# Opening two weight groups at once after each residual step of a two-block transformer kernel

## What is computed

```python
# block 1
n = rmsnorm(h, g_pre_mix);  z = n @ w_in                    # 2048 -> 6592 columns
y = concat(short_conv(z), rwkv7(z));  h = h + rmsnorm(y @ w_out, g_post_mix)
gate, up = split(rmsnorm(h, g_pre_ffn) @ w_gate_up)         # 2048 -> 2 x 5632
h = h + rmsnorm((silu(causal_dwconv(gate)) * up) @ w_down, g_post_ffn)
# block 2
q, k, v = split(rmsnorm(h, g0) @ swa_w_in)                  # 2048 -> 3072
h = h + rmsnorm(attention(q, k, v) @ swa_w_out, g1)
gate, up = split(causal_dwconv(rmsnorm(h, g2) @ ffn_w_up))  # 2048 -> 2 x 5632
out = h + rmsnorm((silu(gate) * up) @ ffn_w_down, g3)
```

## Time and profile before

| what | value |
|---|---|
| median of three runs | 2581.58 us (2580.62 to 2581.98) |
| the profiled execution | 2578.3 us, span 2576.5 us |
| TensorE matmul busy | 2443.8 us, 95% |
| VectorE busy | 1533.0 us, 60% |
| ScalarE busy | 1045.8 us, 41% |
| Pool busy | 131.2 us, 5% |
| DMA | 405.84 MB, mean 158 GB/s |
| mean granted TensorE clock | 0.972 |

### The profile page before, as it was taken

The page is one execution under the profiler, slowest core; times in us unless marked ns, Lnnn a source line. Parts: engine busy times, 40 slices in busy tenths (PEclk is TensorE's granted clock), DMA queues, the critical chain, the costliest instruction groups (busy, mean ns, idle before and its releaser), DMA issues.

```text
span 2576.5 us, 51985 instructions
## 1 busy us (share of the span) xinstructions
PE 2443.8 (95%) x20784; PEld 2290.3 (89%) x20784; DVE 1533.0 (60%) x1989; ACT 1045.8 (41%) x1326; POOL 131.2 (5%) x162
## 2 busy tenths in 40 slices
PE   7989999989999999999999898798999999999996
PEld 7989999888899999998887896377999999998885
DVE  6577555655756665564444745545767767774444
ACT  5433232334544434443444434544444444434442
POOL 2001000001200000000000200002100000000001
PEclk9999999999999999999999897799999999999998
DMA  7434232235455555555565562044555555556653
GB/s 237 155 112 135 92 100 92 84 111 186 140 180 183 183 179 186 180 181 188 189 188 177 188 189 81 1 131 132 168 184 187 187 184 184 181 170 203 188 188 98
DMA packets 116212, 405.84 MB, mean 158 GB/s; under 512 B 12624, under 2 KB 19760, under 8 KB 115824
## 3 DMA queue, kind: packets, MB, share of 16 engines
q1 hardware_dynamic: 109248, 392.22, 47.5%
q10 hardware_dynamic: 6832, 11.68, 1.3%
HBM read 401.69 MB, written 2.15 MB: 157 GB/s over the span
## 4 chain that ended last, share of the span: by engine, by line
PE 84%; issue 6%; DVE 6%; ACT 3%; POOL 0%; ACTq 0%; POOLq 0%; DVEq 0%
PE ps L1494 17%; PE ps L1495 17%; PE ps L1496 16%; PE ps L1490 15%; PE ps L1492 7%; PE ps L1615 3%; PE ps L1604 2%; PE ps L1606 1%; PE ps L1605 1%; PE ps L1825 1%; DVE wl L836 1%; ACT wh L493 1%; DVE h L1277 1%; DVE xl L861 1%; DVE rkr L980 1%
## 5 line engine op out<-in xcount | busy, mean ns | idle before, releaser
L836 DVE TENSOR_TENSOR wl<-raw,wh 128x1024 fp32r<-128x1024 f32 x744 | 912.8, 1235 | 836.1 <-ACT wh L493 835.6
L493 ACT ACTIVATE wh<-raw 128x1024 fp32r<-128x1024 f32 x744 | 782.8, 1058 | 1141.4 <-PE ps L1496 670.8
L1494 PE MATMUL ps<-xh,wh 128*128 128x256 f32 (+2 forms) x3648 | 1040.4, 285 | 56.0 <-DVE xl L861 47.0
L1495 PE MATMUL ps<-xl,wh 128*128 128x256 f32 (+2 forms) x3648 | 1036.4, 284 | 0.0
L1496 PE MATMUL ps<-xh,wl 128*128 128x256 f32 (+2 forms) x3648 | 1035.5, 284 | 0.0
L1494 PEld LDWEIGHTS ps<-xh,wh 128*128 128x128 f32 x3648 | 695.1, 191 | 61.2 <-issue 26.3
L1495 PEld LDWEIGHTS ps<-xl,wh 128*128 128x128 f32 x3648 | 696.7, 191 | 0.2
L1496 PEld LDWEIGHTS ps<-xh,wl 128*128 128x128 f32 x3648 | 694.6, 190 | 0.0
L1490 PE MATMUL ps<-act,wh 128*128 128x512 f32 x1408 | 493.1, 393 | 1.6 <-DVE wl L836 1.6
L1492 PE MATMUL ps<-act,wl 128*128 128x256 f32 x1408 | 392.8, 279 | 0.0
L1490 PEld LDWEIGHTS ps<-act,wh 128*128 128x128 f32 x1408 | 263.8, 187 | 64.4 <-DVE wl L836 1.9
(11 more groups left out here) (228 smaller groups left out, 2064.2 us busy)
## 6 DMA issues: line engine op xcount, KB each, us to landing
raw<-in_gate_up SPq DMA_DIRECT2D x176, 512.0 KB, 3.5
raw<-in_down SPq DMA_DIRECT2D x176, 512.0 KB, 3.7
raw<-in_up SPq DMA_DIRECT2D x176, 512.0 KB, 3.6
raw<-in_w_in SPq DMA_DIRECT2D x104, 512.0 KB, 3.6
raw<-in_in SPq DMA_DIRECT2D x48, 512.0 KB, 3.7
raw<-in_w_out SPq DMA_DIRECT2D x32, 512.0 KB, 3.8
raw<-in_out SPq DMA_DIRECT2D x32, 512.0 KB, 3.6
bias<-bias_rows ACTq DMA_DIRECT2D x1, 4096.0 KB, 29.5
```

The lines of the kernel that those rows point to most:

```text
L493: act.activation(wh[:, slot], raw[:, slot], ACT.Copy).then_inc(high_ready, 1)
L836: dve.tensor_tensor(wl[:, slot], raw[:, slot], wh[:, slot].bitcast(F32), ALU.subtract).then_inc(low_ready, 1)
L1494: pe.matmul(out, w_high, hi, start=(k == 0), stop=False)
L1495: pe.matmul(out, w_high, lo, start=False, stop=False)
```

## The change

After each residual step the first two groups of `gate_up`, `in2` and `up2` are opened together. The host lays their 16 chunks down in the order of `TWO`: pair 0 of group 0, pair 0 of group 1, pair 1 of group 0, and so on for six pairs, then pairs 6 and 7 of group 0, then pairs 6 and 7 of group 1. TensorE's `open_two` follows it, with the sum of squares after chunk 13 of the 16. ScalarE and VectorE make two weight chunks behind each pair of tiles from the third pair on, and one more (chunk 16) before the root and reciprocal. The first steps of `gated`, `upped` and `evacuate_in2` wait for other counts of used chunks, and chunks 17 to 23 are placed between them. Pool multiplies by `rstd_post` tiles 1, 3, 4 and all those behind (14 in place of 8); VectorE keeps tiles 0 and 2. The opening of `w_in` and the last residual step stay as they were.

```diff
+TWO = [(g, c) for c in range(6) for g in range(2)] + [(0, 6), (0, 7), (1, 6), (1, 7)]

 (Pool)
                     scale(1)
                     scale(3)
+                    scale(4)
...
-                    with pool.Fori(1, KT // 2 - 1) as i:
+                    with pool.Fori(1, KT // 2 - 2) as i:
                         scale(2 * i + 3)
+                        scale(2 * i + 4)
                         add(2 * i, 0)
                         add(2 * i + 1, 1)
+                    scale(KT - 1)
+                    add(KT - 4, 0)
+                    add(KT - 3, 1)
                     add(KT - 2, 0)
                     add(KT - 1, 1)

 (ScalarE, opening; VectorE's has lows in place of highs)
-                    if c < 3 and first == 0:
+                    if first:
+                        if c >= 2:
+                            highs(first + 2 * c, 2, 2 * c % RING)
+                        continue
+                    if c < 3:
                         highs(1 + c, 1, 1 + c)
-                    if c >= 3:
-                        highs(first + 4 + c - 3, 1, (c - 3) % RING)
-                highs(first + 9, 3, 1)
-                take_root(name)
+                    else:
+                        highs(4 + c - 3, 1, (c - 3) % RING)
+                if first:
+                    highs(first + 16, 1)
+                    take_root(name)
+                    highs(first + 17, 2, 1)

 (ScalarE, feed_forward)
-                pair(0)
+                gated(0)
+                highs(first + 19, 5, 3)
+                activated(0)
+                highs(first + 24, 4)

 (ScalarE, in2)
-            plain("in2", lambda g: None, skip_first=True)
+            highs(FIRST["in2"] + 19, 1, 3)
+            plain("in2", lambda g: None, skipped=2)

 (VectorE, residual_tile)
-                    if k % 2:
-                        dve.wait_ge(scaled_ready, base // 2 + k // 2 + 1)
+                    if k % 2 if name is None else k not in (0, 2):
+                        turn = base // 16 * (KT - 2)
+                        dve.wait_ge(scaled_ready, turn + (k // 2 + 1 if name is None or k < 4 else k - 1))

 (VectorE, gated; upped is the same with lows 21 and 22 between)
+                    opened = isinstance(p, int) and p == 0
...
-                        lows(p * 16 + (first + 13 + x), 1, 1 + x)
-                    dve.wait_ge(chunk_used, p * 16 + (first + 8))
+                        lows(p * 16 + (first + (17 if opened else 13) + x), 1, 1 + x)
+                    dve.wait_ge(chunk_used, p * 16 + (first + (14 if opened else 8)))

 (VectorE, feed_forward)
-                pair(0)
+                gated(0)
+                lows(first + 19, 2, 3)
+                upped(0)
+                lows(first + 23, 1, 3)
+                split(0)
+                lows(first + 24, 4)

 (VectorE, in2)
-            plain("in2", evacuate_in2, skip_first=True)
+            evacuate_in2(0)
+            lows(FIRST["in2"] + 17, 3, 1)
+            plain("in2", evacuate_in2, skipped=2)

 (TensorE)
+            def open_two(name, moving, n):
+                for x, (g, c) in enumerate(TWO):
+                    at_chunk = FIRST[name] + x
+                    chunks_of(name, at_chunk, at_chunk % RING, g, moving[g], n[g], range(c, c + 1),
+                              None if g else tile_ready(name))
+                    if (g, c) == (0, 7):
+                        square_sum(name)
...
-                group(name, 0, 0, x_of(n), n, tile_ready(name))
-                square_sum(name)
-                group(name, 1, 1, x_up, SEQ)
+                open_two(name, (x_of(n), x_up), (n, SEQ))

 (host; the same for in2 and up2)
+    def opened(w):
+        return np.concatenate([w[[8 * g + c for g, c in TWO]], w[16:]])
```

More of the change, by code:

```diff
@@ L526, in opening @@
                     tile(2 * c + 1)
-                    if c < 3 and first == 0:
-                        highs(1 + c, 1, 1 + c)
-                    if c >= 3:
-                        highs(first + 4 + c - 3, 1, (c - 3) % RING)
-                highs(first + 9, 3, 1)
-                take_root(name)
+                    if first:
[3 more added lines that the diff above has]
+                    if c < 3:
+                        highs(1 + c, 1, 1 + c)
+                    else:
[4 more added lines that the diff above has]
+                    highs(first + 17, 2, 1)
+                else:
+                    highs(9, 3, 1)
+                    take_root(name)
             def mix_group(name, g, src, n):
@@ L555, in mix_group, with plain @@
                     square(src[:, k, :], SQ0[name] + k, n)
-            def plain(name, evacuate, skip_first=False, stops={}, ahead=0):
+            def plain(name, evacuate, skipped=0, stops={}, ahead=0):
                 first, per = FIRST[name], CHUNKS[name]
-                for g in range(1 if skip_first else 0, GROUPS[name]):
+                for g in range(skipped, GROUPS[name]):
                     start = first + g * per + RING
@@ L870, in opening, with plain @@
                         finish()
-                    if c < 3 and first == 0:
-                        lows(1 + c, 1, 1 + c)
-                    if c >= 3:
-                        lows(first + 4 + c - 3, 1, (c - 3) % RING)
-                lows(first + 9, 3, 1)
+                    if first:
+                        if c >= 2:
+                            lows(first + 2 * c, 2, 2 * c % RING)
+                        continue
+                    if c < 3:
+                        lows(1 + c, 1, 1 + c)
+                    else:
+                        lows(4 + c - 3, 1, (c - 3) % RING)
+                if first:
+                    lows(first + 16, 1)
+                else:
+                    lows(9, 3, 1)
                 inverse_root(name, rstd)
-            def plain(name, evacuate, skip_first=False, stops={}, middles={}, ahead=0):
+            def plain(name, evacuate, skipped=0, stops={}, middles={}, ahead=0):
                 first, per = FIRST[name], CHUNKS[name]
-                for g in range(1 if skip_first else 0, GROUPS[name]):
+                for g in range(skipped, GROUPS[name]):
                     start = first + g * per + RING
@@ L902, in group_full @@
             def group_full(name, g):
-                ahead = 4 if (name, g) == ("w_out", 0) else 0
+                ahead = {("w_out", 0): 4, ("in2", 0): 6}.get((name, g), 0)
                 dve.wait_ge(chunk_used, FIRST[name] + (g + 1) * CHUNKS[name] + ahead)
@@ L1779, in _ @@
             down("down", 0)
-            group("in2", 0, 0, x_of(SEQ), SEQ, tile_ready("in2"))
-            square_sum("in2")
-            group("in2", 1, 1, x_of(SEQ), SEQ)
+            open_two("in2", (x_of(SEQ), x_of(SEQ)), (SEQ, SEQ))
             with pe.Fori(1, 3) as i:
@@ L1926 @@
         "ht": hidden.T.reshape(KT, P, L).transpose(1, 0, 2),
-        "w_in": _chunks(np.concatenate(columns, axis=1)), "w_out": w_out, "gate_up": _chunks(gate_up),
-        "down": _chunks(a["w_down"]), "in2": _chunks(in2), "out2": _chunks(out2), "up2": _chunks(up2),
+        "w_in": _chunks(np.concatenate(columns, axis=1)), "w_out": w_out, "gate_up": opened(_chunks(gate_up)),
+        "down": _chunks(a["w_down"]), "in2": opened(_chunks(in2)), "out2": _chunks(out2), "up2": opened(_chunks(up2)),
         "down2": _chunks(a["ffn_w_down_2"][0]),
```

## The result

The changed kernel takes 2556.53 us (median of four runs, 2554.43 to 2558.34), the kernel before beside it 2581.78. The ratio is 0.9902, 95% interval 0.9885 to 0.9919: 25 us less. 2559.3 was forecast. The profiled execution took 2558.0 us, with a span of 2556.2.

A forecast was written before the change was run, and what follows sets the result against it. TensorE, busy 95%, was taken to lose time waiting for xl and to its clock. Recoverable 25.6 less costs 1.1, 1.4 and 0.8 gave 22.3 us, from a median of 2581.6 to 2559.3 us; range 2554 to 2573.

The forecast's parts named there:

- Recoverable: First groups of gate_up, in2 and up2: 8.8, 8.7 and 8.1 us of tile waits and clock loss, together 25.6 us.
- a second fall of the clock: TensorE's clock falling again after waits for tiles inside the first groups; counted within the recoverable 25.6 us.
- Part 1: TensorE's new order of the same 16 chunks and 384 matmuls: cost 0, if tiles and weight chunks keep up.
- Part 2: VectorE's chain in the openings: 6.54 us a pair against TensorE's 5.67, lead nearly enough; cost 1.1 us.
- Part 3: Pool's scale of tile 4 disturbs the first xl: each opening starts 0.45 us later, cost 1.4 us in three.
- Part 4: Behind the opening: chunk 19 waits behind the Silu on ScalarE; cost 0.8 us in up2, 0 in gate_up.
- The sum: Whole kernel: 25.6 - 1.1 - 1.4 - 0.8 = 22.3 us less, giving a median of 2559.3 us.
- the signs named ahead: Trace after: 16-chunk openings of 48 to 49 us, waits for xl about 31 us, clock full from 7 us on.
- Pool holding VectorE four times a pair: Openings: each of Pool's four operations delays VectorE, 7.7 us a pair; about 2573 us, chance 0.26.
- The slower rival: Openings: six collisions a pair, 8.9 us, past the deciding point of 8.5 us; 2592 us, chance 0.04.
- No weight chunk was late in an opening: Rival claiming a weight chunk, not a tile, is late in the openings: 2 us a pair, 2570 us, chance 0.03.

The follow-up runs named there:

- The spare matmuls in the kernel before: Kernel before with ten unused matmuls of 256 columns ahead of each of the last five chunks of the three first groups: 2582.17 us, ratio 1.0002.
- the two kernels with longer pairs: Changed kernel with one or two unused VectorE subtractions more per pair of tiles behind pairs 2 to 6 of each opening: 2571.61 and 2589.23 us.

## Why the prediction was right, point by point

- **Recoverable, 25.6 us.** The three openings gave back 26.7. I took the clock's loss at the start as a cost that stays, 7.0 us, and all else as recoverable. For the sum that holds: after the change the openings are 14 chunks and little else, with 2.1, 1.6 and 2.5 us over (42.4 - 40.3, 41.3 - 39.7, 42.2 - 39.7), and (1 - clock) x length is 2.1, 1.7 and 2.5. So 6.2 us stayed and not 7.0. The 0.8 is in2's start, 1.6 against 2.4 before; it was 2.5 again with Pool's scale late, so this part of the gain is luck and not the change. What was not sound is the reading of the time before, as waits and a second fall of the clock. The spare matmuls in the kernel before took the second fall away, and no group was shorter. The start didn't count there either: its 1.7 to 2.9 us were followed in each group by 4.7 to 6.3 us of waits for xl. So the chain set 33.5 to 33.8 us whatever the clock lost. After the change TensorE sets the length, and there the start of the clock does count, but only 0.9 to 1.1 us of it can be had in gate_up and up2 and nothing in in2, since VectorE's chain stands right behind.
- **Part 1.** Nothing was added: 384 matmuls, the same DMA bytes.
- **Part 2, a pair of 6.54 us and 1.1 us of waits.** The pair and its collisions are in VectorE's and Pool's timelines of in2:

```profile
1417.93 0.94 DVE L882 SCALAR_TENSOR_TENSOR xl<-h,vec,xh 128x256 fp32r<-128x256 f32 x1
...
1440.11 2.90 DVE L857 TENSOR_TENSOR wl<-raw,wh 128x1024 fp32r<-128x1024 f32 x2 [1.44 <-ACT wh L501]
1442.94 0.95 DVE L1306 SCALAR_TENSOR_TENSOR h<-mixf,vec,h 128x256 f32<-128x256 f32 x1
...
1446.51 2.90 DVE L857 TENSOR_TENSOR wl<-raw,wh 128x1024 fp32r<-128x1024 f32 x2 [1.44 <-ACT wh L501]
...
1452.44 2.36 DVE L857 TENSOR_TENSOR wl<-raw,wh 128x1024 fp32r<-128x1024 f32 x2 [1.44 <-ACT wh L501]
```

```profile
1415.90 2.69 POOL L438 TENSOR_TENSOR mixf<-mixf,rstd_post 128x256 f32<-128x256 f32 x3 [61.54 <-DVE rstd_post L876]
...
1440.12 3.49 POOL L438 TENSOR_TENSOR mixf<-mixf,rstd_post 128x256 f32 x2
...
1446.52 1.81 POOL L438 TENSOR_TENSOR mixf<-mixf,rstd_post 128x256 f32<-128x256 f32 x1
```

  1446.51 - 1440.11 = 6.40 us: right to 2%. There are two collisions a pair, as said, though not where: VectorE and Pool alternate, one `wl` is held up (2.90 for two, where 2.36 is undisturbed) and the h behind them (0.95 for 0.47). The cost was nothing and not 1.1, as no wait for xl is listed inside an opening; but it was near, with in2 at tile 11 on its limit. The mis-sized term is the last two pairs: the one at 1446.51 has a single scale beside it and the one at 1452.44 none, while I had charged two and one, so xl of tile 13 ends 36.6 us after the first matmul and not 38.3.
- **Part 3, 0.45 us per start.** The first xl takes 0.94 us in place of 0.47, beside Pool's three scales; the starts are 0.47 us later, and moving the third scale takes that back. Right.
- **Part 4, 0.8 us at chunk 19 of up2, none in gate_up.** 0.73 and none. ScalarE behind the convolution of up2:

```profile
1831.54 1.28 ACT L759 ACT_TABLE_LOAD   x1 [6.32 <-DVE cv L1331]
1832.84 1.06 ACT L759 ACTIVATE sg<-cv 128x1024 f32<-128x1024 f32 x1
1833.80 3.89 ACT L501 ACTIVATE wh<-raw 128x1024 fp32r<-128x1024 f32 x4
```

  Table load and Silu, in the order and at the durations of the earlier trace rows, then `wh`; `wl` follows at 1834.88 and its first 1.2 us are chunk 19's. From the sum's end near 1820.9 that is 15.2 us where 15.0 was worked out. With `wh` put ahead of them the wait is gone.
- **The sum.** 22.3 forecast. By the windows it is 24.6, by the medians 25.3. The chain's 1.1 us and 1.1 of the recoverable time are the difference, and 0.8 of the latter is the chance start of in2. The forecast lay 2.8 us above the median. Of the signs named ahead, the 16 chunks took 48.8, 47.4 and 48.3 us where 48 to 49 stood, and the waits for xl 32.8 us where about 31 stood.
- **The rivals.** Pool holding VectorE four times a pair did not come about: from tile 5 to tile 13 xl stays at 0.47 to 0.48 us, and the squares fall into VectorE's idle 1.44 us, as the later rows of the trace of before had it. The slower rival's six collisions a pair did not come either. Its point, from which the order stops paying, is real: it was put at 8.5 us a pair and lies near 8.4 by the two kernels with longer pairs, with 6.4 in the changed kernel. (Its own sum, 22.3 + 4 x pair against 56.8, gives 8.6; 8.5 is what it gives with the 0.45 us of the later start counted.) No weight chunk was late in an opening before its sum.

By the Trainium skill ("SBUF — State Buffer", section "Who interferes with whom") VectorE and GpSimd contend for a shared port under an exclusive lock, and the one that comes second is fully blocked. The trace agrees: a Pool pair takes 3.49 us beside two `wl`, where a scale alone takes 0.73. The prediction had worked out from this that moving the scales buys VectorE nothing, and the runs say so: 0.9998 with the scales moved alone, 0.9896 with all but them.

## What to carry to other kernels

Where one engine waits for a chain of others tile by tile, ask for how long each tile feeds it: letting a tile serve two groups at once can make a chain that was too slow fast enough, though it has to make a second weight chunk per pair (5.3 us a pair became 6.4, for twice the matmuls). Count the lead that the chain has against its deficit per step, and find the step time at which the reordering stops paying; one dose of extra work on the suspect engine measures it. And when two bounds lie within a microsecond of each other, easing one alone gives less than it is worth: in in2 either alone gave nothing, and both together 0.5 us. In the two other openings the clock alone gave 1 us of the 2.1 and 2.5 that it had cost.

## What the runs showed of the hardware

- Of TensorE's clock: after waits of 4.9 to 5.5 us an opening began at or near 1.2 GHz, and the lost work was 1.7 to 2.9 us before the change, 1.6 to 2.5 after. Twenty matmuls that ended 2.3 to 3.0 us before the first tile kept it up in one opening of three, 36 that ended 0.5 to 1.1 us before it in all nine openings of three kernels.
- The same code in w_in had the clock at 0.98 and at 0.94 over 150 us in two executions, 6.5 us apart. The attention stretch (clock 0.70 to 0.72) took 115.8 to 118.6 us over fourteen profiles, from reading `vf` to the first matmul of out2. It was 118.3 before and 115.9 after the change; as it varies like this among kernels that are the same there, I don't count these 2.4 us as the change's, and why the clock falls differently there stays open.
